# Long and short matmuls of a weight chunk: one column block at a time instead of both per k tile

## The reference

```
for layer in range(2):
    hn  = rms_norm(h, mix_norm[layer])
    mix = attention(hn, ...) if layer == 0 else rglru_block(hn, ...)
    h   = h + mix
    h   = h + square(relu(rms_norm(h, mlp_norm[layer]) @ w_up[layer])) @ w_down[layer]
return rms_norm(h, final_norm)
```

## Time and profile before

| | |
|---|---|
| median of 3 runs | 1999.37 us (1999.22 to 1999.66) |
| profiled execution | 1999.79 us, span 1998.0 us |
| TensorE busy | 1978.7 us (99%) |
| weight loads | 1732.5 us (87%) |
| VectorE, ScalarE busy | 1371.9 us (69%), 1061.3 us (53%) |
| mean granted TensorE clock | 0.996 |
| DMA | 368.17 MB, mean 184 GB/s |

### The profile page before, as it was taken

The page is one execution under the profiler, slowest core; times in us unless marked ns, Lnnn a source line. Parts: engine busy times, 40 slices in busy tenths (PEclk is TensorE's granted clock), DMA queues, the critical chain, the costliest instruction groups (busy, mean ns, idle before and its releaser), DMA issues.

```text
span 1998.0 us, 33893 instructions
## 1 busy us (share of the span) xinstructions
PE 1978.7 (99%) x11492; PEld 1732.5 (87%) x11492; DVE 1371.9 (69%) x1577; ACT 1061.3 (53%) x1445; POOL 7.3 (0%) x11
## 2 busy tenths in 40 slices
PE   9999999999999999999999999999999999999997
PEld 8898888888888888888888888888888888888886
DVE  7998676556656665666789997766566556656665
ACT  6666554444444444445588885544444444444453
POOL 1000000000000000000000000000000000000000
PEclk9999999999999999999999999999999999999998
DMA  8434565566555655556566656565656565656552
GB/s 285 158 127 158 171 197 187 192 188 190 189 189 177 198 188 186 177 178 197 189 190 189 189 169 198 181 197 190 190 179 195 188 190 184 197 181 190 188 179 84
DMA packets 365883, 368.17 MB, mean 184 GB/s; under 512 B 11536, under 2 KB 363920, under 8 KB 365712
## 3 DMA queue, kind: packets, MB, share of 16 engines
q1 hardware_dynamic: 365552, 365.53, 57.6%
q0 software_dynamic: 288, 2.10, 0.3%
HBM read 365.48 MB, written 2.10 MB: 184 GB/s over the span
## 4 chain that ended last, share of the span: by engine, by line
PE 93%; DVE 4%; ACT 2%; issue 1%; DMA 0%; DVEq 0%; SPq 0%; ACTq 0%
PE ps L1279 61%; PE ps L1282 30%; DVE w_lo L791 1%; ACT h L454 1%; PE aux L1299 1%; PE aux L1300 1%; PE aux L1301 1%; ACT w_hi L357 0%; DVE h L902 0%; DMA h<-x_l_dram 0%; DVE h L913 0%; DVE u L805 0%; DVE h L1264 0%; PE aux L1354 0%; DVE pt L918 0%
## 5 line engine op out<-in xcount | busy, mean ns | idle before, releaser
L791 DVE TENSOR_TENSOR w_lo<-w_raw,w_hi 128x1024 fp32r<-128x1024 f32 x678 | 816.0, 1222 | 337.9 <-ACT w_hi L357 336.7
L357 ACT ACTIVATE w_hi<-w_raw 128x1024 fp32r<-128x1024 f32 x678 | 701.4, 1053 | 450.1 <-PE ps L1282 446.8
L1279 PE MATMUL ps<-xn,w_hi 128*128 128x512 f32 x2880 | 907.5, 396 | 2.7 <-DVE xn L859 2.4
L1279 PE MATMUL ps<-mid,w_hi 128*128 128x512 f32 x2544 | 799.5, 396 | 1.1 <-DVE w_lo L791 0.5
L1282 PEld LDWEIGHTS ps<-xn,w_lo 128*128 128x128 f32 x2880 | 541.7, 188 | 128.1
L1282 PEld LDWEIGHTS ps<-mid,w_lo 128*128 128x128 f32 x2544 | 477.9, 188 | 113.0
L1282 PE MATMUL ps<-xn,w_lo 128*128 128x256 f32 x2880 | 566.8, 278 | 0.0
L1282 PE MATMUL ps<-mid,w_lo 128*128 128x256 f32 x2544 | 500.0, 278 | 0.0
L1279 PEld LDWEIGHTS ps<-xn,w_hi 128*128 128x128 f32 x2880 | 439.6, 189 | 3.7 <-issue 3.1
L1279 PEld LDWEIGHTS ps<-mid,w_hi 128*128 128x128 f32 x2544 | 387.2, 189 | 1.8 <-DVE w_lo L791 0.9
L805 DVE TENSOR_TENSOR u<-ps,half 128x512 f32<-128x512 f32 x170 | 117.3, 690 | 161.2 <-ACT half L370 141.8
(11 more groups left out here) (154 smaller groups left out, 751.6 us busy)
## 6 DMA issues: line engine op xcount, KB each, us to landing
w_raw<-mlp_w_up_dram SPq DMA_DIRECT2D x256, 512.0 KB, 3.8
w_raw<-mlp_w_down_dram SPq DMA_DIRECT2D x256, 512.0 KB, 3.5
w_raw<-b_w_in_dram SPq DMA_DIRECT2D x64, 512.0 KB, 5.0
w_raw<-a_w_qkv_dram SPq DMA_DIRECT2D x40, 512.0 KB, 5.3
w_raw<-a_w_o_dram SPq DMA_DIRECT2D x32, 512.0 KB, 4.5
w_raw<-b_w_out_dram SPq DMA_DIRECT2D x32, 512.0 KB, 4.6
h<-x_l_dram SPq DMA_DIRECT2D x4, 512.0 KB, 8.4
gate_raw<-b_gate_a_w_dram SPq DMA_DIRECT2D x8, 256.0 KB, 2.8
```

Source lines behind the costliest of these rows:

```text
L357: nc.scalar.activation(w_hi[:, s, :, :], w_raw[:, slot, :, :], ACT.Copy).then_inc(hi_ready, 1)
L791: nc.vector.tensor_tensor(w_lo[:, s, :, :], w_raw[:, slot, :, :], w_hi[:, s, :, :].bitcast(F32), ALU.subtract).then_inc(lo_ready, 1)
L1279: nc.tensor.matmul(ps[:, 2 * half_i + b, :], hi[:, k, b * PART:(b + 1) * PART], operand[:, :, kt, :], start=kt == 0, stop=False)
```

## The change

Per chunk the loops are exchanged. Before, the k tile is the outer loop, and for each k tile come the long matmuls of column blocks 0 and 1, then their short ones. After, the column block is the outer loop, and for each k tile come its long and then its short matmul. The matmuls, their operands and destinations, the waits ahead of them and the signal behind the last are the same.

```
-                for k in range(CH_KT):
-                    kt = s * CH_KT + k
-                    for b in range(2):
-                        nc.tensor.matmul(ps[:, 2 * half_i + b, :], hi[:, k, b * PART:(b + 1) * PART],
-                                         operand[:, :, kt, :], start=kt == 0, stop=False)
-                    for b in range(2):
-                        last = nc.tensor.matmul(ps[:, 2 * half_i + b, TOK:2 * TOK], lo[:, k, b * PART:(b + 1) * PART],
+                for b in range(2):
+                    cols = slice(b * PART, (b + 1) * PART)
+                    for k in range(CH_KT):
+                        kt = s * CH_KT + k
+                        nc.tensor.matmul(ps[:, 2 * half_i + b, :], hi[:, k, cols], operand[:, :, kt, :],
+                                         start=kt == 0, stop=False)
+                        last = nc.tensor.matmul(ps[:, 2 * half_i + b, TOK:2 * TOK], lo[:, k, cols],
                                                 operand[:, 0, kt, :], start=False, stop=kt == KT - 1)
                 last.then_inc(wts_used, 1)
```

## The result

The changed kernel takes **2021.24 us** (median of 4 runs, 2020.89 to 2021.28) against 1999.49 us before (4 runs): ratio 1.011, 95% interval 1.0098 to 1.0122. That is 21.75 us slower; no change was forecast, and 2018 was the top of the range. The profiled execution has a span of 2019.5 us, 21.5 more than the earlier trace rows.

A forecast was written before the change was run, and what follows sets the result against it. The prediction took TensorE's own matmul queue as the bound. Its three terms, 0 + 0 + 0 on the profiled 1999.79 us, with the runs' median 0.4 below, gave 1999.4 us, range 1985 to 2018.

The forecast's parts named there:

- What bounds the kernel: TensorE's own queue sets the end; 696.7 ns per four matmuls, 154 us in all not streaming columns.
- Step 1: Weight loads on TensorE: spreading short matmuls' loads recovers nothing, term 0; bounds -5.0 and -56.7 ns per four matmuls.
- Step 2: PSUM writes: eight matmuls in a row into one bank, shorts onto columns just written, cost 0; other end +25 us.
- rival A: Each short behind its own long pays 4.6 ns for the repeated PSUM region: +25 us, 2024 us; chance 0.10.
- Step 3: TensorE's order: four changes of length per four matmuls instead of two; taken as 0, ends 0 and +5.0 ns.
- Rival B: A toll on each change of length in TensorE's stream: +5.0 ns per four matmuls, +13.6 us, 2013 us; chance 0.15.
- Rival C: TensorE's mixed stream loses its surplus over the gates: -5.0 ns per four matmuls, -13.6 us, 1986 us; chance 0.13.
- Rival D: TensorE's weight loader runs further ahead once no long follows a long: -154 us, 1846 us; chance 0.04.
- What hides the rest: ACT and DVE splits and DMA stay hidden behind TensorE; earlier completion of column block 0 frees nothing.

The follow-up runs named there:

- e3: Against the changed kernel, each chunk takes all 8 long matmuls, then its 8 shorts, column blocks in turn; 2003.2 us, ratio 1.0019 to the kernel before.
- e1: Against the changed kernel, two longs then their two shorts within a column block, all in one PSUM bank; 1999.52 us, ratio 1.000 to the kernel before.
- e2: Against the changed kernel, long and short alternate between the column blocks' banks in three chunks of four; 2021.3 us, ratio 1.0108 to the kernel before.
- e6: Changed kernel plus three unused runs of the 24 gate matmuls in the second layer's channel mixer; 2016.73 us, ratio 1.0086 to the kernel before.
- e5: Changed kernel plus 24 unused short matmuls into an idle bank behind the statistics of each channel mixer's first half; 2026.72 us, 1.0136.
- b2: Changed kernel plus 6 unused short matmuls in each channel mixer, behind the chunk that follows the statistics; 2021.98 us, ratio 1.0116.
- b3: Changed order only in attention, LRU stage behind its first block and channel mixers, with 24 unused matmuls per mixer; order of before elsewhere; 2023.91 us, 1.0124.
- f2: Changed kernel plus 24 unused matmuls once per channel mixer, with the gates' weight pattern and the mixer's activations; 2027.22 us, ratio 1.0142.
- e6b: Changed kernel plus three unused runs of 24 matmuls in the second layer's channel mixer, on that mixer's own activations and weights; 2016.5 us, 1.0085.
- g1: Changed order only in attention, LRU stage behind its first block and both channel mixers, with 12 unused matmuls per mixer; order of before elsewhere; 1995.15 us, 0.9977.
- e8: Changed kernel with every short matmul widened to 512 columns, so one length only, more work and another result; 2564.91 us (one run).

## Why the prediction was wrong

*What bounds the kernel.* Right: TensorE's own queue, 696.7 ns a group, 154 us of excess, and "the excess is all that an order of the same matmuls can touch". All of the 21.5 us is there.

*Step 1, the load under each matmul.* This is the step that failed: "a matmul's turn depends only on its own length and the one load under it. Then the sum is the same", and the term is 0. A turn depends on the turns before as well. The loader does work one ahead and starts with the running matmul, after as before, but that does not make the turns independent: a long takes 230 ns on the lower level and 236 on average on the upper one, and 227 to 236 within one chunk of e3. The step gave bounds for a gain alone (-5.0 and -56.7 ns a group) and none for a loss; measured is +10.0 ns a group on the upper level and -3.3 on the lower. The gates were the right row to look at and were read halfway: their 12.9 is the average of a run that starts unsettled, the settled turn has 13.3 over its columns. That is the floor of a stream of one length, and it says nothing on what a mix pays above it.

*Step 2, the PSUM region.* 0 was right (e1, e2), and rival A wrong, though its 2024 came nearer to 2021.24 than the forecast did. Its marks, shorts at 119 or more and longs at 233, are not in the trace: on the upper level shorts have 117 on average (113, 117 and 120 in turns), longs 236.

*Step 3, changes of length.* The cause lies here in so far as the rhythm of lengths decides. Rival B had the sign and missed size and form: 10.0 and not 5.0 ns a group, and not in proportion to the changes, since e3 got slower with fewer.

*Rival C* gave 692 ns a group if the surplus goes. That is close to the lower level, 693.3, on which 90 chunks of the changed kernel ran. It was priced for all chunks, and the choice between it and the upper level was no part of the working.

*Rival D* did not come. The Trainium skill says that TensorE can pull weight loads ahead of running matmuls ("TensorE: Matmul & The Clock Gate", Part 2). The traces agree for one load, which starts with the running matmul, and show no more: no run has a load that starts before the matmul ahead of its own. The same page ("Back-to-back issue gap") gives N / 2.4 + 2.5 ns, as the gap of an isolated matmul; no settled stream of one-pass float32 matmuls here comes to that, the best is N / 2.4 + 13.3.

*What hides the rest* held: no new wait, the same DMA share.

**Open.** That alternating lengths make the pace, and that it has two levels, is shown; why is not. Which part of the chip holds the memory of the pace isn't known. The upper level repeats over three pairs (long turns of 232, 236 and 241 ns), as two periodic things do that slip against each other; that is an argument, not a finding. Also open is the full rule of entry. Behind a run settled at 120 ns the alternating stream was on the lower level each time, and it had come from the upper one in the gates, attention and e6. One that had not settled led to the upper level in e5, b2, b3 and f2, and to the lower one in e6b. And the lower level came without any run in the first block of e5 and e6b, and in e5 from 1001 us on, right behind the statistics. So a settled run has been enough so far; it is not necessary, and other entries were not controlled.

## What to carry to other kernels

In this kernel TensorE is the bound and each matmul carries its own weight load, and the order of long and short matmuls moved the time by about 1% through the turns alone. In a kernel of this kind, measure start to start over a long stretch, at several places of the trace: one order can have more than one pace. An order that is neutral in counts, loads and waits need not be neutral in time, and the forecast for it needs a term of either sign. If a stage runs at the better pace elsewhere in the same trace, look at what stood ahead of it there, and test with a control whether that is what brought it.

## What the runs showed of the hardware

- A settled stream of one-pass float32 matmuls of one length, each with its load, takes its columns at 2.4 GHz plus 13.3 ns: 120.0 ns at 256 columns, 226.8 at 512 (e8).
- Mixed lengths take 13.3 to 16.7 ns over their columns, by rhythm: in pairs 14.2, in eights 14.6, in turns 13.3 or 16.7.
- The pace of alternating lengths lasts: over 600 us in e6 and g1, through loop ends and from one operand to the other. In the changed kernel it changed behind a wait of 0.39 us at 1197.30, and without any wait at 194.30 and 1212.74, where a chunk with weights in other tiles ended.
- Behind a change of length turns settle step by step: eight longs in a row take 233, 236, 228, 233, 231, 227, 227, 227 ns (e3).
- The same code can enter on either level: in the first block e5 and e6b were on the lower, the changed kernel and four others on the upper.
- Weight loads run one ahead: no load starts before the matmul ahead of its own.
- Adding 72 unused matmuls (8.7 us) made the changed kernel 4.5 us faster (e6).
